# A decoder layer on 8 cores: the norm's scaling of tiles 8 to 15 on GpSimd, a new hand-written order, more zero products

## The chip, the cores and the metric

One Trainium2 chip, 8 cores, each with the same program on its own share of the data; the cores exchange nothing. The metric is the device time in microseconds of the slowest core. TensorE's clock has two levels in the records of this kernel, 1.2 and 2.4 GHz; the granted clock is given as a share of 2.4.

## The reference

One layer of a hybrid decoder on a prompt batch (8 sequences of 2048 tokens, one per core) and on a sample batch (128 sequences of 4 tokens, 16 per core), D = 1024:

```
h   = rmsnorm(x) * (1 + scale1) + shift1          # scale, shift, gate = silu(c) @ w_ada + b_ada
[v_pool | x_conv | B | C] = h @ w_in              # 4 x 512 columns
y_A = groupwise(mean_window(v_pool) - v_pool)     # windows 2, 4, 8, 16
y_B = B * dwconv3(C * x_conv)
x   = x + gate1 * rmsnorm([y_A | y_B] @ w_out)
h2  = rmsnorm(x) * (1 + scale2) + shift2
[a | b] = dwconv3(h2 @ w_up)                      # 2 x 2816 columns
x   = x + gate2 * rmsnorm((silu(a) * b) @ w_down)
```

The outputs are x and the last rows of the pooling, convolution and feed-forward inputs. All is float32 at the interface.

## The kernel before

A core holds its 2112 tokens as 17 tiles: 16 of 128 tokens and tile 16 with 64 sample tokens. Products are bfloat16 with float32 sums in PSUM, which has 8 banks of 512 columns.

**The first norm (T:t).** `tile_in(t)` calls `x_front(t)`, which loads x in pairs of tiles (1 MB, `load_pair`, on SP's queue; three pair buffers taken in turn, and a fourth place for the pair of tile 6), and `norm_tile` (L708). `stats` (L687) squares the tile on ScalarE with a sum, takes the root on ScalarE and the reciprocal on VectorE. Then the tile is scaled by it into a bfloat16 buffer: tiles 0 to 7 on VectorE (L730), tiles 8 to 16 on ScalarE (L728). `turn_tile` (L744) transposes the eight 128 x 128 blocks on TensorE into one PSUM bank, and VectorE or ScalarE copies them to AH, the transposed input of all projections. Buffers of the scaled tile: seven for tiles 0 to 7 (`xn` by t % 7), three for the others (t % 3).

**The start.** The scale vector's weights and the pooling columns of w_in come in 8 pieces (`scp`, 0.79 MB each at the source, cast by GpSimd's DMA queue). `a:kc` (`scale_in`) multiplies piece kc's part with silu(c) on TensorE, and VectorE makes the scale G1T of it. `s:kc,c` (`start_step`) applies it on VectorE to one block of 512 tokens (tiles 4c to 4c+3) and issues 4 (c = 0) or 3 (c = 1) start products of 512 columns (L856) that sum over kc in seven PSUM banks. These seven banks are held until s:7,c; tiles 0 to 2 and 4 to 6 are turned in the banks that c = 1 uses later, all others and every `a` take the one bank that is left, in the order of the list.

**The rest up to the output projection.** `O:g,c` copies a start bank out; `P:g,c` is a pooling projection of 8 products for a block of 512 tokens, `W:g,c` its window sums on VectorE; `m:j,c` issues the 24 products of a convolution unit (weights `ring<-w_inc`, 1.57 MB at the source), `v:j,c` its elementwise part, `U` both. `S` makes shift1 from four loads of 1 MB (`wsh`), `M:c` applies G1T to blocks 2 and 3, `A`, `g`, `G`, `Y`, `w` belong to the second modulation, the gates and the load of w_out, `F` folds the pooling map into w_out. Then `o_step` runs the output projection, and after it the feed-forward part.

**What sets the order.** The list PROJ (L48) says in which order these steps are recorded. That fixes the banks and buffers, and with them who waits for whom. `Sched.order` (L149) then plays the program through with written costs (DMA at 315e3 bytes per us, L144) and fixes each engine's queue: among what is ready, the lowest place in the list as TensorE uses it goes first. Loads are issued by the same rank, limited by the bytes in flight (L147); up to 70 us of the plan a load also waits for the load that had landed last when the plan issued it. All queues are in order on the chip: SP holds x loads, GpSimd the cast weight loads and its own arithmetic.

**Zero products.** `keep_warm` (L275) puts products with a tile of zeros ahead of a TensorE step that waits 0.5 us or more in the plan, up to 110 us: 0.85 of the gap, at 0.2139 us each (`PAD`, `FILL`, L273). They go to the bank that the step is about to write, as far as it has been freed, and wait for nothing that comes late. The start has 24 of them. The start product's padding (L861) exists as for other steps.

Each engine's queue is written out by `emit` (L307).

Of the kernel before, what the change touches and what calls it, by code (L numbers as in the profile page):

```python
# [12 lines left out]
ALU = mybir.AluOpType  # L13
# [3 lines left out]
KC = 8  # L17
T = 2048
# [74 lines left out]
class Sched:  # L93
# [176 lines left out]
                done(o)  # L270
        self.makespan = t

    PAD, FILL, PADDED = 0.2139, 0.85, 110.0  # L273

    def keep_warm(self, zeros):  # L275


        t = 0.0
        for o in self.ops["pe"]:
            gap, end = o.start - t, t  # L280
            t = o.start + o.cost
            if o.pad is None or gap < 0.5 or o.start > self.PADDED:
                continue
            late = {d for d in o.deps if d.end > end + 0.25 and d not in o.full}
            o.early = [d for d in o.deps - late if d.eng != "pe"] + [zeros]
            gap = o.start - max([end] + [d.end + self.HOP[d.eng] for d in o.full])
            o.pads = max(0, int(self.FILL * gap / self.PAD)) if end else self.FIRST
            zeros.need = True

    def finalize(self, esems, zeros):  # L290
        self.order()
        self.keep_warm(zeros)
        for o in self.all:
            if o.eng == "pe":
# [41 lines left out]
def build_program():  # L336
# [68 lines left out]
    STAT = alloc("stat", [128, 8, 18], F32)  # L405
# [50 lines left out]
    ZERO = alloc("zero", [128, 512], BF16)  # L456
# [36 lines left out]
    R = Region  # L493
# [369 lines left out]
    def tile_in(t):  # L863
        x_front(t)
# [790 lines left out]
```

How the kernel before makes its waits and increments, by code:

```python
    def emit(self, eng, e):  # L306
        waited = {}
        def wait(deps):
            need = {}
            for d in deps:
                s, v = d.sig
                if need.get(s, 0) < v:
                    need[s] = v
            for s, v in need.items():
                if waited.get(s, 0) < v:
                    e.wait_ge(s.h, v)
                    waited[s] = v
        for o in self.ops[eng]:
            if o.pads:
                wait(o.early)
                for _ in range(o.pads):
                    o.pad(e)
            wait(o.deps)
            if o.fn is None:
                continue
            r = o.fn(e)
            if o.dma:
                assert len(r) == o.n, (len(r), o.n)
                for i in r:
                    i.then_inc(o.sem.h, 16)
            elif o.need:
                r.then_inc(o.sig[0].h, 1)
```

## Time and profile before

| | |
|---|---|
| runs of the kernel before | 714.68, 716.30, 716.55 us, median 716.3 |
| the profiled execution | 716.71 us |
| its span, slowest core (core 1) | 715.2 us; the cores 710.0 to 715.2 |
| granted TensorE clock of the cores | 0.990 to 0.998 |
| busy: TensorE, VectorE, ScalarE, GpSimd | 691.9, 454.2, 318.9, 230.3 us |
| HBM read and written | 127.02 and 20.63 MB |

The profile is that of one execution on its slowest core; times in it are counted from the start of the span. The execution's own time is 1.5 us longer than the span. "PE" is TensorE's products, "PEld" its weight loads, "DVE" VectorE, "ACT" ScalarE, "POOL" GpSimd. Products are pipelined, so a group's time has the tail of its last product in it, and neighbouring groups overlap by some 0.17 us. The size in a line of the DMA view is that written to SBUF; a cast load reads twice as much.

### The profile page before, as it was taken

Reading aid. Unit: us, or ns where it says so; the run is one execution under the profiler, and the core shown is the slowest. Engines: PE = TensorE matmul, PEld = TensorE weight load, DVE = VectorE, ACT = ScalarE, POOL = GpSimd, SP = SyncE. Lnnn points to the kernel's source line nnn. Section 1 sums busy time; section 2 is a strip of 40 time slices with the busy share of each in tenths; the row PEclk is TensorE's granted clock in tenths of the full one; section 3 lists DMA queues with packets and bytes.
Section 4 is the critical chain, followed back from the end, with each engine's and each line's share of the span. In section 5 each row is a group of like instructions: output and inputs, shape, how many; then the busy total and the mean of one; then the engine's idle time right before and its main releaser. Section 6 shows DMA issues by size and latency. Waiting matters only on the chain.

```text
span 715.2 us, 11905 instructions; the slowest of 8 cores (710.0 to 715.2 us)
## 1 busy us (share of the span) xinstructions
PE 691.9 (97%) x4022; PEld 329.2 (46%) x4022; DVE 454.2 (64%) x612; ACT 318.9 (45%) x600; POOL 230.3 (32%) x231
## 2 busy tenths in 40 slices
PE   6889999999899999999999999999999999999996
PEld 2435544444444444444444444454444444444443
DVE  2729599664688787777777333157777777769303
ACT  4258654334576864444444211154444445423111
POOL 1100012000777743344444222214324242323320
PEclk8999999999999999999999999999999999999998
DMA  8998879999998579358999968103244333062322
GB/s 233 213 230 140 204 133 172 163 176 177 216 236 307 188 132 164 60 110 143 156 158 162 221 194 266 60 31 74 51 95 78 60 59 60 1 238 98 127 88 75
DMA packets 31980, 102.81 MB, mean 144 GB/s; under 512 B 11632, under 2 KB 12144, under 8 KB 27056
## 3 DMA queue, kind: packets, MB, share of 16 engines
q0 software_dynamic: 9072, 47.71, 39.8%
q1 hardware_dynamic: 22848, 54.33, 25.1%
q8 instruction: 33, 0.54, 0.3%
q14 instruction: 27, 0.22, 0.1%
HBM read 127.02 MB, written 20.63 MB: 206 GB/s over the span
## 4 chain that ended last, share of the span: by engine, by line
PE 90%; issue 3%; DVE 2%; ACT 2%; POOL 1%; DMA 1%; DVEq 0%; SPq 0%; ACTq 0%; POOLq 0%
PE ps L541 84%; PE ps L856 2%; PE ps L551 1%; PE ps L534 1%; PE ps L559 1%; DMA big<-x 1%; DVE big L576 1%; POOL big L580 1%; ACT xnp L572 1%; DVE ah L757 1%; POOL e L580 0%; ACT big L572 0%; DVE stat L691 0%; ACT stat L572 0%; ACT L572 0%
## 5 line engine op out<-in xcount | busy, mean ns | idle before, releaser
L541 PE MATMUL ps<-ah,ring 128*128 128x512 bf16 (+2 forms) x2240 | 405.3, 342 | 1.6 <-DVE big L576 0.8
L541 PEld LDWEIGHTS ps<-ah,ring 128*128 128x128 bf16 x2240 | 188.2, 98 | 212.5 <-issue 4.3
L576 DVE SCALAR_TENSOR_TENSOR big<-ps,misc,big 128x1023 f32<-128x1023 f32 (+1 forms) x176 | 224.9, 1282 | 73.2 <-ACT halo L572 30.7
L580 POOL TENSOR_TENSOR g<-big 128x1024 bf16<-128x1024 f32 x44 | 104.5, 2375 | 173.6 <-DVE big L580 96.3
L572 ACT ACTIVATE big<-ps,misc 128x1024 f32<-128x1024 f32 x88 | 97.9, 1114 | 139.8 <-PE ps L541 139.8
L541 PE MATMUL ps<-wdn,g 128*128 128x512 bf16 (+2 forms) x726 | 153.1, 373 | 0.0
L541 PEld LDWEIGHTS ps<-wdn,g 128*128 128x128 bf16 x726 | 69.9, 98 | 81.1 <-issue 0.4
L580 POOL TENSOR_TENSOR big<-big 128x256 f32<-128x256 f32 (+2 forms) x35 | 52.9, 1522 | 110.7 <-DVE big L576 97.1
L572 ACT ACTIVATE big<-ps 128x1024 bf16<-128x1024 f32 (+4 forms) x31 | 29.0, 937 | 122.8 <-PE ps L541 106.6
L691 DVE RECIPROCAL stat<-stat 128x1 f32<-128x1 f32 (+1 forms) x64 | 9.9, 159 | 96.3 <-ACT stat L572 96.0
L541 PE MATMUL ps<-wo,by 128*128 128x512 bf16 x256 | 57.0, 379 | 1.4 <-DVE stat L691 1.4
L572 ACT ACTIVATE big<-big 128x1024 f32<-128x1024 f32 x44 | 46.5, 1056 | 4.3 <-DVE big L580 3.3
L541 PEld LDWEIGHTS ps<-wo,by 128*128 128x128 bf16 x256 | 24.6, 98 | 30.2 <-issue 2.3
L591 POOL DMA_DIRECT2D ring<-w_up x22 | 12.8, 581 | 75.8 <-PE ps L541 75.8
L576 DVE SCALAR_TENSOR_TENSOR big<-ps,stat,gtp 128x1024 f32<-128x1024 f32 x26 | 33.3, 1281 | 5.4 <-PE ps L541 3.3
L576 DVE SCALAR_TENSOR_TENSOR ta<-q,misc,ta 128x512 f32<-128x512 f32 x32 | 23.7, 748 | 7.8 <-ACT q L572 2.6
L572 ACT ACTIVATE junk<-big 128x1024 bf16<-128x1024 f32 (+1 forms) x15 | 15.7, 1049 | 20.0 <-DMA big<-x 20.0
L534 PE MATMUL ps<-zero 128*128 128x512 bf16 x74 | 21.0, 428 | 3.7 <-DVE zero L602 1.9
L572 ACT ACTIVATE stat<-stat,eps 128x1 f32<-128x1 f32 (+1 forms) x64 | 17.4, 291 | 2.5 <-ACT big L572 0.4
L541 PE MATMUL ps<-ah,scp 128*128 128x512 bf16 (+1 forms) x104 | 18.0, 322 | 0.0
L587 DVE TENSOR_SCALAR ah<-ah,g2t,s2t 128x512 bf16<-128x512 bf16 x32 | 15.4, 541 | 2.9 <-DMA ah<-xnp 2.9
L580 DVE TENSOR_TENSOR tsa<-usb,misc 128x1408 f32<-128x1408 f32 x6 | 13.6, 2273 | 5.6 <-ACT usb L572 5.4
(150 smaller groups left out, 461.1 us busy)
## 6 DMA issues: line engine op xcount, KB each, us to landing
ring<-w_up POOLq DMA_DIRECT2D x22, 1024.0 KB, 10.0
y<-big SPq DMA_DIRECT2D x23, 512.0 KB, 2.8
big<-y SPq DMA_DIRECT2D x16, 512.0 KB, 4.7
big<-x SPq DMA_DIRECT2D x7, 1024.0 KB, 8.0
wdn<-w_down POOLq DMA_DIRECT2D x11, 512.0 KB, 12.2
wg<-w_gate POOLq DMA_DIRECT2D x4, 1024.0 KB, 15.7
big<-x SPq DMA_DIRECT2D x8, 512.0 KB, 11.1
scp<-w_scp POOLq DMA_DIRECT2D x8, 384.0 KB, 7.1
```

Source lines behind the costliest of these rows:

```text
L534: o.pad = lambda e: e.matmul(ap, ZERO[:, 0:ap.shape[0]], ZERO[:, 0:n], start=first, stop=first)
L541: inst = e.matmul(bank_ap, l, r, start=(first and i == 0), stop=(last and i == len(pairs) - 1))
L551: inst = e.matmul(o, ls[i], r, start=(i == 0), stop=(i == len(ls) - 1))
L559: inst = e.transpose(o, i, ident)
L572: return K.op("act", lambda e: e.activation(out=out, in_=in_, func=func, **kw), reads=reads, writes=writes, cost=c_act(n, ptr))
L576: return K.op("dve", lambda e: e.scalar_tensor_tensor(out, in0, s, in1, op0, op1), reads=reads, writes=writes, cost=c_dve(n), port=not any ...
L580: return K.op(eng, lambda e: e.tensor_tensor(out, in0, in1, op), reads=reads, writes=writes, cost=c_dve(n) if eng == "dve" else c_pool(n), ...
L587: return K.op("dve", lambda e: e.tensor_scalar(out, in0, s1, s2, op0, op1), reads=reads, writes=writes, cost=c_dve(n, mode), port=mode > 1.0)
L591: return K.dma(eng, lambda e: [e.dma_start(out=dst, in_=src)], sem or next_misc(), 1, reads=reads, writes=regs, deps=deps, nbytes=nbytes)
L691: K.op("dve", lambda e: e.reciprocal(STAT[0:rows, k + 1, t:t + 1], STAT[0:rows, k + 1, t:t + 1]), reads=[r_stat[k + 1][t]], writes=[r_stat ...
L757: K.op("dve", lambda e: e.tensor_copy(AH[:, :, r0:r0 + rows], psb[:, :, 0:rows]), reads=[r_bank[b]], writes=regs, cost=c_dve(KC * rows, 2.0))
L856: inst = e.matmul(PSF[:, start_b[g, c], :], WINP[kc][:, g * 128:(g + 1) * 128], AH[:, kc, c * 512:(c + 1) * 512], start=(kc == 0), stop=(k ...
```

## The change

It does four things. The scaling of tiles 8 to 15 goes from ScalarE to GpSimd (tile 16 stays on ScalarE). The list PROJ is another one. A second play-through, `retime`, keeps the order of the queues and sets the planned times anew with slower DMA (295e3 bytes per us) and 0.05 us more for each hand-over between engines; the number of zero products follows from these times. `keep_warm` fills 0.9 of a gap in place of 0.85, and between s:0,0 and s:7,0 it fills every planned gap of 0.35 us or more, ahead of any TensorE step, with zero products that are added to the first start bank and wait for nothing but the zeros.

```diff
 PROJ = """
-T:0 T:1 T:2 a:0 T:6 T:3 T:7 T:4 a:1 T:5 a:2 s:0,0 s:1,0 a:3 a:4 s:0,1 s:2,0 a:5 T:8 s:1,1 s:3,0 s:2,1 s:4,0
-s:3,1 T:9 a:6 a:7 s:5,0 s:6,0 s:7,0 s:4,1 O:1,0 s:5,1 O:0,0 s:6,1 s:7,1 T:10 m:0,1 T:11 O:2,0 O:2,1 T:16 M:2 K
-m:0,0 W:0,0 T:12 W:2,0 S O:3,0 W:1,0 m:0,4 O:1,1 P:3,1 O:0,1 W:3,0 v:0,0 P:2,2 P:0,2 W:2,1 m:1,0 I T:13 T:14
-m:1,4 v:1,0 m:0,2 W:3,1 P:1,2 T:15 W:1,1 v:0,1 M:3 P:3,2 v:0,2 m:1,1 W:0,1 Z W:2,2 W:1,2 v:1,1 m:0,3 P:1,3 N
...
+T:0 T:1 T:2 T:10 T:11 T:3 a:0 T:6 T:14 s:0,0 T:12 a:1 a:2 T:7 T:4 a:3 a:4 s:1,0 T:5 T:13 s:0,1 s:2,0 a:5 a:6
+s:3,0 s:1,1 s:2,1 a:7 s:4,0 s:5,0 s:6,0 s:3,1 s:7,0 K O:2,0 W:2,0 O:0,0 s:4,1 T:15 m:0,0 s:5,1 O:1,0 s:6,1 T:16
+s:7,1 T:8 T:9 O:2,1 O:1,1 W:1,0 O:3,0 S m:0,4 P:3,1 W:2,1 M:2 W:3,0 O:0,1 m:1,4 v:0,0 m:0,1 P:1,2 P:2,2 W:0,0
+M:3 m:0,3 P:0,2 C m:1,0 v:1,0 Y:1 W:0,1 v:0,1 m:0,2 I v:0,2 Y:0 W:1,1 P:0,3 m:1,1 v:1,1 W:2,2 N W:3,1 v:0,4
...
 """
+XPOOL = tuple(range(8, 16))
...
+    SLOW, LATE = 295e3, 0.05
+
+    def retime(self):
...
-    PAD, FILL, PADDED = 0.2139, 0.85, 110.0
+    PAD, FILL, PADDED = 0.2139, 0.9, 110.0
 
     def keep_warm(self, zeros):
...
         t = 0.0
+        hot = None
         for o in self.ops["pe"]:
             gap, end = o.start - t, t
             t = o.start + o.cost
+            if o is self.hot[1]:
+                hot = None
+            if o is self.hot[0]:
+                hot = self.hot[2]
+            elif hot is not None and gap >= 0.35:
+                o.pad, o.early, o.pads = hot, [zeros], int(self.FILL * gap / self.PAD)
+                zeros.need = True
+                continue
...
         self.order()
+        self.retime()
         self.keep_warm(zeros)
...
-        if k == ST1 and t > 7:
+        if k == ST1 and t in XPOOL:
+            K.op("pool", lambda e: e.tensor_scalar(N[0:rows, :], X[0:rows, :], STAT[0:rows, k + 1, t:t + 1], None, ALU.mult),
+                 reads=[r_x, r_stat[k + 1][t]], writes=[r_n], cost=1.3)
+        elif k == ST1 and t > 7:
             act(N[0:rows, :], X[0:rows, :], AF.Copy, [r_x, r_stat[k + 1][t]], [r_n], D, scale=STAT[0:rows, k + 1, t:t + 1])
...
-        return padded(o, PSF[:, start_b[gs[0], c], :], 512, kc == 0)
+        padded(o, PSF[:, start_b[gs[0], c], :], 512, kc == 0)
+        if c == 0 and kc in (0, KC - 1):
+            hot.append(o)
...
+    K.hot = hot + [lambda e: e.matmul(PSF[:, start_b[0, 0], :], ZERO[:, 0:128], ZERO, start=False, stop=False)]
     K.finalize(esems, zeros)
```

The later lines of the list differ too; the weights of the second modulation, of w_out and the last convolution units keep their place behind the first 100 us.

## Rows read from the trace of the kernel before

**Rows 1.** The page: its span and TensorE's busy time.

```profile
span 715.2 us, 11905 instructions; the slowest of 8 cores (710.0 to 715.2 us)
...
PE 691.9 (97%) x4022; PEld 329.2 (46%) x4022; DVE 454.2 (64%) x612; ACT 318.9 (45%) x600; POOL 230.3 (32%) x231
```

**Rows 2.** Stretches: window, length, busy PE, PEld, DVE, ACT, POOL, granted clock, DMA share, GB/s.

```profile
40.50:54.57 14.07, 11.19 (x68) 5.39 (x67) 3.42 (x10) 7.30 (x13) 1.05 (x2) 0.88 1.01 246
54.57:95.60 41.03, 40.31 (x354) 21.80 (x353) 31.31 (x67) 30.26 (x67) 3.26 (x7) 1.00 0.80 152
95.60:169.80 74.20, 74.13 (x505) 35.76 (x506) 56.70 (x100) 31.45 (x85) 6.01 (x13) 1.00 0.99 175
```

**Rows 3.** The same view for the zero products alone (PE, PEld).

```profile
9.00:54.57 45.57, 14.13 (x50) 4.96 (x50) 0.89 1.02 226
```

**Rows 4.** TensorE's timeline, core 1: start, duration, operation, [idle before <- releaser].

```profile
40.55 3.40 PE L534 MATMUL ps<-zero 128*128 128x512 bf16 x15
43.78 0.61 PE L559 MATMUL ps<-idb,xn 128*128 128x128 bf16 x8
...
45.55 0.61 PE L559 MATMUL ps<-idb,xn 128*128 128x128 bf16 x8
47.43 0.34 PE L541 MATMUL ps<-sc,scp 128*128 128x18 bf16 x8 [1.27 <-ACT ah L572]
...
48.79 4.87 PE L856 MATMUL ps<-ah,scp 128*128 128x512 bf16 x14
...
54.57 0.61 PE L559 MATMUL ps<-idb,xn 128*128 128x128 bf16 x8
55.02 5.34 PE L541 MATMUL ps<-ah,ring 128*128 128x512 bf16 x24
...
85.35 1.89 PE L541 MATMUL ps<-ah,ring 128*128 128x512 bf16 x8 [0.70 <-DVE bias L1023]
```

**Rows 5.** Loads: when issued (timelines of GpSimd and SP), then us to landing (DMA view).

```profile
33.83 0.53 POOL L591 DMA_DIRECT2D scp<-w_scp  x1 [1.69 <-DMA scp<-w_scp]
39.33 0.53 POOL L591 DMA_DIRECT2D ring<-w_inc  x1 [4.98 <-DMA scp<-w_scp]
...
36.66 0.33 SPq L591 DMA_DIRECT2D big<-x  x1
...
scp<-w_scp POOLq DMA_DIRECT2D x1, 384.0 KB, 7.4
...
big<-x SPq DMA_DIRECT2D x1, 1024.0 KB, 7.5
ring<-w_inc POOLq DMA_DIRECT2D x1, 768.0 KB, 9.8
```

**Rows 6.** ScalarE's timeline: the square and the scaling of tile 8.

```profile
36.68 1.06 ACT L572 ACTIVATE junk<-big 128x1024 bf16<-128x1024 f32 x1 [12.83 <-DMA big<-x]
...
39.32 1.15 ACT L572 ACTIVATE xn<-big,stat 128x1024 bf16<-128x1024 f32 x1
```

**Rows 7.** TensorE's timeline of core 2: the last start products, first products of m:0,0.

```profile
47.01 3.18 PE L856 MATMUL ps<-ah,scp 128*128 128x512 bf16 x14
...
51.56 4.70 PE L541 MATMUL ps<-ah,ring 128*128 128x512 bf16 x21
```

**Rows 8.** TensorE's waits on other engines, 55 to 170 us: total, times, longest.

```profile
PE ps L541 <- DVE bias L1023: 0.7, 1, 0.7
```

**Rows 9.** Groups of instructions by shape: busy us, mean ns, idle before.

```profile
L572 ACT ACTIVATE xn<-big,stat 128x1024 bf16<-128x1024 f32 x8 | 9.2, 1146 | 1.2 <-DVE stat L691 1.1
...
L585 DVE TENSOR_SCALAR xn<-big,stat 128x1024 bf16<-128x1024 f32 x6 | 4.2, 747 | 0.0
...
L580 POOL TENSOR_TENSOR g<-big 128x1024 bf16<-128x1024 f32 x44 | 104.5, 2375 | 173.6 <-DVE big L580 96.3 <-DVE big L576 69.8 <-DVE hc L580 4.1
L580 POOL TENSOR_TENSOR big<-big 128x1024 f32<-128x1024 f32 x14 | 36.5, 2604 | 94.7 <-DVE big L576 84.6 <-DMA big<-y 10.1
```

**Rows 10.** The tile view of g2t: ns min/median/max of the modulations beside GpSimd's additions.

```profile
L587 DVE TENSOR_SCALAR ah<-ah,g2t,s2t x32: 388/402/1391, 204.1 to 435.6; 128x512 bf16<-128x512 bf16 x32
```

More of the change, by code:

```diff
@@ L48 @@
 PROJ = """
-T:0 T:1 T:2 a:0 T:6 T:3 T:7 T:4 a:1 T:5 a:2 s:0,0 s:1,0 a:3 a:4 s:0,1 s:2,0 a:5 T:8 s:1,1 s:3,0 s:2,1 s:4,0
-s:3,1 T:9 a:6 a:7 s:5,0 s:6,0 s:7,0 s:4,1 O:1,0 s:5,1 O:0,0 s:6,1 s:7,1 T:10 m:0,1 T:11 O:2,0 O:2,1 T:16 M:2 K
-m:0,0 W:0,0 T:12 W:2,0 S O:3,0 W:1,0 m:0,4 O:1,1 P:3,1 O:0,1 W:3,0 v:0,0 P:2,2 P:0,2 W:2,1 m:1,0 I T:13 T:14
-m:1,4 v:1,0 m:0,2 W:3,1 P:1,2 T:15 W:1,1 v:0,1 M:3 P:3,2 v:0,2 m:1,1 W:0,1 Z W:2,2 W:1,2 v:1,1 m:0,3 P:1,3 N
-W:3,2 P:2,3 m:1,2 W:2,3 W:1,3 v:0,3 W:0,2 C Y:1 Y:0 P:0,3 v:1,2 W:0,3 P:3,3 R v:0,4 L W:3,3 W:1,4 m:1,3 v:1,3 B
-W:3,4 A:6 U:2,4 A:7 w U:2,0 U:3,4 U:2,1 U:3,0 U:3,1 A:1 A:0 A:2 U:3,2 U:2,2 g v:1,4 W:2,4 U:3,3 A:4 A:5 A:3 G
-W:0,4 F U:2,3
+T:0 T:1 T:2 T:10 T:11 T:3 a:0 T:6 T:14 s:0,0 T:12 a:1 a:2 T:7 T:4 a:3 a:4 s:1,0 T:5 T:13 s:0,1 s:2,0 a:5 a:6
+s:3,0 s:1,1 s:2,1 a:7 s:4,0 s:5,0 s:6,0 s:3,1 s:7,0 K O:2,0 W:2,0 O:0,0 s:4,1 T:15 m:0,0 s:5,1 O:1,0 s:6,1 T:16
+s:7,1 T:8 T:9 O:2,1 O:1,1 W:1,0 O:3,0 S m:0,4 P:3,1 W:2,1 M:2 W:3,0 O:0,1 m:1,4 v:0,0 m:0,1 P:1,2 P:2,2 W:0,0
+M:3 m:0,3 P:0,2 C m:1,0 v:1,0 Y:1 W:0,1 v:0,1 m:0,2 I v:0,2 Y:0 W:1,1 P:0,3 m:1,1 v:1,1 W:2,2 N W:3,1 v:0,4
+P:2,3 W:1,2 P:3,2 g W:3,2 v:1,4 R P:1,3 P:3,3 W:0,2 Z L A:6 v:0,3 W:1,3 m:1,2 v:1,2 W:3,3 U:2,4 U:2,0 A:3 m:1,3
+A:7 W:3,4 U:2,1 v:1,3 W:0,3 U:2,2 U:3,4 U:2,3 A:2 W:2,3 U:3,0 A:0 U:3,1 B W:1,4 A:1 A:5 W:0,4 U:3,2 w F A:4
+W:2,4 G U:3,3
 """
@@ L271, in order, with push, done @@
         self.makespan = t
-    PAD, FILL, PADDED = 0.2139, 0.85, 110.0
+    SLOW, LATE = 295e3, 0.05
+    def retime(self):
+        users = {o: [] for o in self.all}
+        wait = {o: len(o.deps) for o in self.all}
+        for o in self.all:
+            for d in o.deps:
+                users[d].append(o)
+        turn = {e: 0 for e in self.ENGS}
+        busy = {e: False for e in self.ENGS}
+        queue = {"sp": [], "pool": []}
+        events = []
+        seq = [0]
+        port = [0.0, 0.0]
+        t = 0.0
+        ready = {o for o in self.all if not wait[o]}
+        left = len(self.all)
+        def push(at, kind, o):
+            seq[0] += 1
+            heapq.heappush(events, (at, seq[0], kind, o))
+        def done(o):
+            o.end = t
+            for u in users[o]:
+                wait[u] -= 1
+                if not wait[u]:
+                    push(t + (0.0 if o.eng == u.eng == "pe" else self.HOP[o.eng] + self.LATE), "ready", u)
+        while left:
+            for e in self.ENGS:
+                if busy[e] or turn[e] >= len(self.ops[e]) or self.ops[e][turn[e]] not in ready:
+                    continue
+                o = self.ops[e][turn[e]]
+                turn[e] += 1
+                busy[e] = True
+                o.start = t
+                c = o.cost
+                if o.dma:
+                    push(t + c, "free", o)
+                    continue
+                if o.port:
+                    c += max(0.0, port[e != "pool"] - t)
+                    port[e == "pool"] = t + c
+                push(t + c - self.OVER[e], "free", o)
+                push(t + c, "done", o)
+            live = [q for q in queue.values() if q]
+            nxt = events[0][0] if events else 1e9
+            head = None
+            rows = sum(q[0][0].row for q in live)
+            for q in live:
+                f = t + q[0][1] * rows / (self.SLOW * q[0][0].row)
+                if f <= nxt:
+                    nxt, head = f, q
+            for q in live:
+                q[0][1] -= (nxt - t) * self.SLOW * q[0][0].row / rows
+            t = nxt
+            if head is not None:
+                push(t + self.DMA_OUT, "landed", head.pop(0)[0])
+                continue
+            _, _, kind, o = heapq.heappop(events)
+            if kind == "ready":
+                ready.add(o)
+            elif kind == "free":
+                busy[o.eng] = False
+                left -= 1
+                if o.dma:
+                    push(t + self.DMA_IN, "moving", o)
+            elif kind == "moving":
+                queue[o.eng].append([o, float(o.nbytes)])
+            else:
+                done(o)
@@ L281, in keep_warm @@
             t = o.start + o.cost
+            if o is self.hot[1]:
[5 more added lines that the diff above has]
+                zeros.need = True
+                continue
             if o.pad is None or gap < 0.5 or o.start > self.PADDED:
@@ L848, in start_weights @@
         load(SCP[kc], wsp_d[kc], [r_scp[kc]], 3 << 18, eng="pool")
+    hot = []
     def start_mm(kc, c):
```

## The prediction

> **What bounds the kernel now.** I first read the page: TensorE is busy for 691.9 of 715.2 us [rows 1]. The time is TensorE's instruction stream plus what is lost in it, so a change in the order pays only where TensorE runs zero products, waits, or runs at the lower clock. The stretches say where that is [rows 2]: from 95.6 to 169.8 us TensorE is busy for 74.13 of 74.20 us, from 54.57 to 95.6 us 0.7 us are missing, while the last 14 us before 54.57 hold 2.9 us of idle time at a granted clock of 0.88. The zero products lie in the same place: 50 of them with 14.13 us between 9 and 54.57 us [rows 3]. What the change can win lies before 55 us, some 0.7 us of it behind.
>
> TensorE's timeline shows how the stretch ends [rows 4]. 15 zero products run from 40.55 us, the transposes of T:8 start at 43.78, those of T:9 at 45.55, and only then a:6 at 47.43. a:6 itself was long ready: scp 7, the last of its kind, was issued at 33.83 and took 7.4 us, so it was there at 41.2 [rows 5]. It waited because T and a share the one PSUM bank that the start products leave free, in the order of the list, and T:8, T:9 stand ahead of it. T:8 is late because its x pair landed at 36.7 us (ScalarE had waited 12.83 us for it) and its tile was scaled at 40.47 [rows 6]; the 15 zero products then held it for 3.3 us more. The 14 start products after that took 4.87 us, in core 2 3.18 us: they ran at the 1.2 GHz level for a part of it, after the gaps of 44 to 48.8 us. Core 2 started its first product of m:0,0 at 51.56 us and core 1, the slowest, at 55.02 [rows 4, 7]; their spans are the 710.0 and 715.2 us of the page.
>
> **The new order.** T:10 to T:14 come ahead of a:7, and T:8, T:9 behind s:7,1. The bank chain of a:6 and a:7 then hangs on x pairs loaded early, so the stop of 40.5 to 48.8 us cannot recur in this form. But seven pairs of x (0, 2, 10, 6, 14, 12, 4) now land before scp 7, where it was five and part of a sixth.
>
> What the transfers allow: by 41.2 us had landed misc 0.24 MB, five x pairs of 1.05 MB, eight scp of 0.79 MB (f32 at the source) and some 0.63 MB of the pair issued at 36.66 (7.5 us) [rows 5]: 12.4 MB in 40.1 us, 0.309 MB/us. The same sum to the landing of w_inc (39.33 + 9.8 us = 49.1) gives 15.1 MB in 48.0 us, 0.314. I take 0.312. In the new order scp 7 makes 13.87 MB, so 46 us; a:7, its VectorE steps and the last seven start products take about 3 us, which is 49. m:0,0 needs w_inc 0 too: 15.44 MB, with the samples' tile and half of the pair of T:8 moving beside it (0.8 MB, as its neighbours did before) 16.24 MB: 52.1 + 1.1 = 53.1 us. T:15 and T:16 fill 0.8 us of the time between.
>
> The terms, for core 1:
> - m:0,0 starts at 53.1 in place of 55.0 us: -1.9. The cold start products are in this, for TensorE has slack before w_inc lands.
> - By then 14 tiles and the samples are turned, before only T:0 to T:10. Three tiles at 0.45 us (54.57 to 55.02 us [rows 4]) and, my estimate from that, 0.35 for the samples: -1.7.
> - The 0.70 us wait at 85.35 [rows 4] was for a bank that VectorE freed late, beside T:14. T:14 is gone from there: -0.7.
> - More zero products. They run for 0.9 of each planned gap, with a plan that moves 0.295 MB/us, 5.5% under my measured 0.312. Where the data comes earlier than planned they hold real work, as the 15 did. At 16.24 MB the plan is 3.0 us behind, of which 0.9 are filled: the bound is 2.7 us, the other end 0 (TensorE waits anyway and stays warm). I take +0.5, nearer to 0 since w_inc's landing and not TensorE ends this stretch.
> - ScalarE loses eight scalings of 1.146 us, 9.2 in all [rows 9]. Between 55 and 170 us TensorE's one wait is the 0.7 us on VectorE, none is on ScalarE [rows 8], so this is worth nothing; what hides it is TensorE's full stream.
> - GpSimd gains eight scalings, which no row shows. VectorE does one in 0.747 us, GpSimd's own products of 1024 columns take 2.375 and 2.604 us [rows 9]; I take 2.4, the same engine and output type. Six of them (tiles 10 to 15) fall before 49 us, between the scp loads of the same queue. A load in flight covers 7.4 us, so I put the delay at nothing; without that cover it is the second rival.
>
> The pair of T:4 now waits for the buffer of 10 and 11, which GpSimd frees: landing at 18 to 19 us plus two scalings is 25 us, and the transfers reach that pair (9.94 MB) only at 33 us. T:4 can start about 37 us. From there to 47 us TensorE has some 9.6 us of real work for 10 us: tight, and the first place where the forecast can slip. VectorE, SP's queue and the output projection see the same work earlier, at no cost that I can name; behind 170 us nothing changes but the start.
>
> GpSimd's price by the Trainium skill, GPSIMD Engine Reference, section 3.1, would be smaller: its two-input products stand at a port floor that one-input work escapes, down to 1.8 cycles per element, an estimate of 1.5 us for 1024. The trace agrees with the two-input figure only (2.375 us); no row has the other. By it six scalings are 9 us, and the second rival loses most of its price.
>
> Sum: -1.9 - 1.7 - 0.7 + 0.5 = -3.8 us. The profiled execution took 716.7 us (span 715.2 and 1.5 around it), so 712.9; it lies 0.4 above the median of 716.3, so **712.5 us**. About 0.3%, 2.1 us, is what a measurement of this kernel can tell from no change.
>
> **Rivals.**
> 1. Zero products eat it. The plan's slower transfers are obeyed by real instructions: +2.7 in place of +0.5 gives a gain of 1.6, 714.7 us. For it: both groups of zero products that I looked at ran on after their tile was ready. Against it: the last wait is a load. Chance 0.18.
> 2. The GpSimd queue. Loads stand behind scalings that wait for x and for VectorE's reciprocal. Six scalings of 2.4 us, 14.4, less the cover of 7.4 us, put scp 7 and w_inc 0 7.0 us later: m:0,0 at 60.1 us, 5.1 later than now, less 2.4 for the tiles and the bubble: 2.7 us slower, 719.0 us. It decides from 4 us of idle transfers before 50 us. Chance 0.15.
> 3. The shared port. One VectorE scaling of 512 columns took 1391 ns where the shortest took 388, beside GpSimd's adds [rows 10]: 1.0 us of blocking. Eight new GpSimd instructions could each cost a VectorE step on the chain that; if half of them hit, 4.0 us: 716.5 us. Chance 0.06. The Trainium skill, SBUF — State Buffer, section Who interferes with whom, states this as a rule (the port pair is locked for a whole instruction, the second one blocks fully), and the trace agrees [rows 10]; before the output projection the old kernel had no GpSimd arithmetic to collide with.
> 4. The loads arrive better than that: w_inc 0 not slowed by its neighbours (15.44 MB, 50.6 us) and no pad held: 3.0 us more gain, 709.5 us. Chance 0.07.
> 5. The planner reorders, and the list comes out much as before: 716.3 us, 0.02. The bank chain follows the list itself, which speaks against it.
>
> **How the numbers follow.** The forecast has 0.52, with its own range of 710.5 to 714.1. Faster by over 0.3% is 0.52 + 0.07, within 0.3% 0.18 + 0.06 + 0.02, slower 0.15. The range reaches from below the fourth rival to just inside the second: 708.5 to 718.
>
> **What would show it.** Right: a:6 and a:7 within 2 us of scp 7's landing at 46 us; no half-clock stretch between 20 and 55 us; m:0,0 at 53 us with 14 tiles turned; more than 60 zero products before 55 us; no TensorE wait at 85 us; GpSimd scalings of 1.5 to 2.5 us. Wrong: TensorE standing before T:4 beyond 38 us, idle transfers before 50 us, VectorE steps of over 1 us, or new gaps between 55 and 170 us, which would give the gain back where it is full now.

## The result and the profile after

The changed kernel took 729.7 us (median of 4 runs, 728.7 to 731.2) against 716.3 us for the kernel before: a ratio of 1.018 (95% interval 1.016 to 1.020), 13 us slower. The forecast was 712.5 us, 3.8 us faster. In some executions, whatever the kernel, the cores of one die show a lower granted clock and the time is some per cent longer; the ratios leave these out. The page and the groups by shape of the changed kernel, slowest core (core 2):

```profile
span 727.7 us, 11911 instructions; the slowest of 8 cores (717.0 to 727.7 us)
PE 696.1 (96%) x3974; PEld 332.6 (46%) x4049; DVE 458.7 (63%) x612; ACT 312.2 (43%) x592; POOL 254.6 (35%) x239
L815 POOL TENSOR_SCALAR xn<-big,stat 128x1024 bf16<-128x1024 f32 x8 | 23.6, 2956 | 17.6 <-DVE stat L778 15.0
```

Against [rows 1] TensorE is busy 4 us longer and idle 8 us longer. GpSimd's scaling takes 2.96 us in the mean. That is more than the 2.4 us that I took, and more than the 2.604 us of its slowest product [rows 9]. The stretches say where TensorE loses time; the columns are those of [rows 2]:

```profile
24.00:40.50 16.50, 11.72 (x79) 6.39 (x82) 5.50 (x13) 4.17 (x9) 9.88 (x7) 0.79 0.81 169
40.50:54.57 14.07, 12.25 (x112) 6.51 (x113) 10.80 (x26) 6.16 (x13) 8.53 (x8) 1.00 0.70 113
54.57:70.00 15.43, 14.19 (x85) 6.74 (x85) 10.89 (x29) 8.99 (x19) 2.08 (x4) 1.00 0.79 174
169.80:215.00 45.20, 40.27 (x203) 18.41 (x206) 23.43 (x36) 22.15 (x49) 19.25 (x26) 0.92 0.75 142
```

Two places stand out. From 40.5 to 54.57 us the DMA share is 0.70 where it was 1.01 [rows 2], and from 169.8 to 215 us TensorE is idle for 4.9 us and has a clock of 0.92. From 24 us on the DMA share is lower as well. The kernel before had these two lines (core 1), and was idle for 2.9 us in the second:

```profile
24.00:40.50 16.50, 13.66 (x120) 7.25 (x119) 8.88 (x26) 3.66 (x7) 2.77 (x7) 1.00 1.05 202
169.80:215.00 45.20, 42.26 (x230) 20.06 (x229) 28.22 (x48) 26.31 (x58) 28.21 (x38) 1.00 1.01 214
```

**The first place, before m:0,0.** The chain of waits of the changed kernel from 24 us on (start, duration, what), cut to its long pieces:

```profile
26.95 13.83 DMA big<-x
...
40.86 1.20 ACT junk L659 x3
...
44.66 1.05 ACT junk L659 x2
...
46.36 1.04 PE ps L948 x4
...
47.45 1.76 POOL xn L815
...
50.78 2.90 POOL xn L815
53.68 9.40 DMA ring<-w_inc
63.08 0.14 issue
63.22 0.81 PE ps L628 x3
```

It reads backwards: m:0,0 starts at 63.22 us, when w_inc 0 has landed; that load was issued at 53.68, when the last two scalings were done. GpSimd's timeline of the same core shows who stands ahead of whom:

```profile
20.34 5.67 POOL L815 TENSOR_SCALAR xn<-big,stat 128x1024 bf16<-128x1024 f32 x2 [10.17 <-DVE stat L778]
25.97 1.12 POOL L678 DMA_DIRECT2D scp<-w_scp  x2
...
44.31 0.53 POOL L678 DMA_DIRECT2D scp<-w_scp  x1 [1.25 <-DMA scp<-w_scp]
47.45 6.28 POOL L815 TENSOR_SCALAR xn<-big,stat 128x1024 bf16<-128x1024 f32 x2 [2.61 <-PE ps L948]
53.68 0.58 POOL L678 DMA_DIRECT2D ring<-w_inc  x1
```

GpSimd delays the loads at two points. The scalings of tiles 10 and 11 hold its queue until 26.0 us, and the next two scp loads stand behind them: they go out at 24.3 to 26.0 us in the eight cores, where the first of them goes out at 21.1 to 22.4 when GpSimd scales nothing (13). Later the last pair of scalings starts at 47.45 us and takes 6.28, and w_inc 0, issued at 39.33 before [rows 5], goes out 14.4 us later, at 53.68. In all cores it goes out at 51.4 to 53.7.

What the last pair waited for differs. In core 2, the slowest, the x pair of T:4 landed late, at 40.8 us, the statistics of the last tiles stood behind those of T:4 in ScalarE's queue, and the chain above goes through them. In the seven other cores the pair starts at 45.2 to 46.3 us. In cores 0, 3, 5 and 6 ScalarE had the last statistics done by 40.9 to 42.3, and the scalings waited for VectorE's reciprocals. In core 0 these stood in VectorE's queue behind a step that waited 1.44 us for TensorE's `a`:

```profile
43.21 0.29 DVE L674 TENSOR_SCALAR g1t<-ps,vd,misc 128x17 f32<-128x17 f32 x1 [1.44 <-PE ps L628]
...
44.81 0.22 DVE L778 RECIPROCAL stat<-stat 128x1 f32<-128x1 f32 x2
```

The x load of T:4 was not held up by the buffer that GpSimd frees: it goes out at 26.7 to 27.6 us in all cores, and at 28.2 to 29.3 when GpSimd scales nothing (13).

The DMA view of 10 to 64 us in 40 slices of 1.35 us (busy tenths, then GB/s) has both holes:

```profile
DMA  7999999999940699999998793699998000899998
GB/s 261 358 292 165 273 290 316 370 340 340 340 158 0 73 164 132 163 199 229 266 244 171 70 203 59 91 125 155 148 203 160 5 0 5 118 197 255 256 352 364
```

Nothing moves from 26.2 to 27.5 us, and almost nothing from 51.9 to 55.9 us, around the issue of w_inc 0.

**GpSimd once more, at T:9.** The scalings of tiles 8 and 9 come behind s:7,1, and TensorE waits for the second of them:

```profile
71.46 5.97 POOL L815 TENSOR_SCALAR xn<-big,stat 128x1024 bf16<-128x1024 f32 x2
77.58 0.61 PE L646 MATMUL ps<-idb,xn 128*128 128x128 bf16 x8 [2.40 <-POOL xn L815]
```

Every core has this wait of 2.3 to 2.6 us. Where GpSimd scales nothing, or only half the columns, it is not there.

**The second place, the output projection.** TensorE's timeline in core 2, then SP's:

```profile
178.32 10.52 PE L628 MATMUL ps<-wo,by 128*128 128x512 bf16 x47
193.57 9.99 PE L628 MATMUL ps<-wo,by 128*128 128x512 bf16 x32 [4.72 <-DVE stat L778]
```

```profile
176.71 0.33 SPq L678 DMA_DIRECT2D e<-x  x1
177.68 0.81 SPq L1277 DMA_DIRECT2D gtp<-gate_scratch  x2
178.53 3.21 SPq L1279 DMA_DIRECT2D gts<-gate_scratch  x2
```

The gate is loaded at 177.68 us, 0.64 us ahead of the first output product (before: issued at 167.09 in core 1, 2.7 us ahead). VectorE needs it for the first residual, so it waits 8.2 us, the PSUM banks stay taken, and TensorE stands 4.72 us. Behind the stall 32 products take 9.99 us, 0.31 each, where 47 took 10.52 before it: the granted clock from 193.57 to 203.5 us is 0.70, so it was at the 1.2 GHz level for a part of them. Two things hold the load back. The new list puts A:4 behind F, and the gate lies over the buffer of A:4's weights; and in SP's queue it stands behind the load `e<-x`. They were lifted together (6), so how much each costs is not shown. The first output product itself comes at 175.5 to 180.4 us, before at 167.3 to 169.8.

The cores split by this stall without any experiment: 0, 5 and 6 have none there and spans of 717.0 to 718.7 us; 1, 2, 3, 4 and 7 stand 1.7 to 4.7 us and have 724.3 to 727.7.

### The profile page after: what moved, and what is told of

Its sections match the earlier page's. It is cut to its first block, busy times and chain, and to the rows that moved or that the text cites. A ratio compares the mean times of both kernels' runs of the same rounds, so it can differ in the third digit from the quotient of the medians.

```text
span 727.7 us, 11911 instructions; the slowest of 8 cores (717.0 to 727.7 us)
## 1 busy us (share of the span) xinstructions
PE 696.1 (96%) x3974; PEld 332.6 (46%) x4049; DVE 458.7 (63%) x612; ACT 312.2 (43%) x592; POOL 254.6 (35%) x239
## 4 chain that ended last, share of the span: by engine, by line
PE 79%; DMA 8%; issue 4%; DVE 3%; ACT 3%; POOL 2%; SPq 0%; DVEq 0%; ACTq 0%; POOLq 0%
PE ps L628 77%; DMA big<-x 4%; DMA gts<-gate_scratch 2%; DVE big L663 1%; DMA ring<-w_inc 1%; DMA scp<-w_scp 1%; PE ps L638 1%; POOL xn L815 1%; DVE ah L674 1%; ACT big L659 1%; ACT junk L659 0%; POOL big L667 0%; ACT xnp L659 0%; PE ps L646 0%; ACT stat L659 0%
## 5 line engine op out<-in xcount | busy, mean ns | idle before, releaser
L667 POOL TENSOR_TENSOR big<-big 128x256 f32<-128x256 f32 (+2 forms) x35 | 52.9, 1519 | 110.2 <-DVE big L663 96.4
L628 PE MATMUL ps<-wo,by 128*128 128x512 bf16 x250 | 59.2, 393 | 5.0 <-DVE stat L778 4.7
L678 POOL DMA_DIRECT2D ring<-w_up x22 | 12.8, 582 | 70.5 <-DMA gts<-gate_scratch 53.1
L815 POOL TENSOR_SCALAR xn<-big,stat 128x1024 bf16<-128x1024 f32 x8 | 23.6, 2956 | 17.6 <-DVE stat L778 15.0
L646 PE MATMUL ps<-idb,xn 128*128 128x128 bf16 (+1 forms) x140 | 12.0, 238 | 11.6 <-POOL xn L815 6.1
L847 DVE COPY ah<-ps 128x1024 bf16<-128x1024 bf16 (+1 forms) x17 | 11.4, 670 | 16.8 <-PE ps L646 16.7
L621 PE MATMUL ps<-zero 128*128 128x512 bf16 (+1 forms) x61 | 18.0, 454 | 2.9 <-DVE zero L689 1.9
```

The lines of the kernel that those rows point to most:

```text
L621: o.pad = lambda e: e.matmul(ap, ZERO[:, 0:ap.shape[0]], ZERO[:, 0:n], start=first, stop=first)
L628: inst = e.matmul(bank_ap, l, r, start=(first and i == 0), stop=(last and i == len(pairs) - 1))
L646: inst = e.transpose(o, i, ident)
L667: return K.op(eng, lambda e: e.tensor_tensor(out, in0, in1, op), reads=reads, writes=writes, cost=c_dve(n) if eng == "dve" else c_pool(n), ...
L678: return K.dma(eng, lambda e: [e.dma_start(out=dst, in_=src)], sem or next_misc(), 1, reads=reads, writes=regs, deps=deps, nbytes=nbytes)
L815: K.op("pool", lambda e: e.tensor_scalar(N[0:rows, :], X[0:rows, :], STAT[0:rows, k + 1, t:t + 1], None, ALU.mult), reads=[r_x, r_stat[k + ...
```

## The experiments

Theory A: GpSimd's scaling delays m:0,0. Theory B: the late gate load costs the rest. Rivals: the zero products; the loss of ScalarE's part; the new list itself. "The order as it stands" below means that the planner's result for the changed kernel is written into the kernel, so that every queue keeps its order. "o" is the first output product, "up" the first up-projection product; the time between is 60.8 us when TensorE stands nowhere in it.

**1. The new list without GpSimd.**

```diff
-XPOOL = tuple(range(8, 16))
+XPOOL = ()
```

> The changed kernel with tiles 8 to 15 scaled by ScalarE again; GpSimd's queue is then the same list of loads with the eight scalings taken out. Theory A (loads wait behind scalings in GpSimd's queue): m:0,0 starts at 53 to 55 us instead of 60.6 to 63.3, DMA share back to 0.95 or more between 24 and 54 us, total 718 to 721 us, since the late gate load at the output projection stays. Rival B (the new order of the x pairs is itself to blame): m:0,0 still at 59 us or later and the total above 725 us. Rival C (zero products): the same as B, for they stay.

Ratio 1.013 (1.011 to 1.015). m:0,0 comes at 55.7 to 57.8 us, some 5 us earlier than with GpSimd. But TensorE stood 0.4 to 4.0 us on the weights `w_ss` at 131 to 137 us in every core, and 0.8 to 4.1 us at the output projection in five cores; the three that did not stand there (1, 2 and 5) have spans of 713.1 to 713.8 us. GpSimd is a part, not all.

**2. GpSimd's scaling in the old list.**

```diff
+        if k == ST1 and t > 7 and t < 16:
+            K.op("pool", lambda e: e.tensor_scalar(...), ..., cost=1.3)
```

> The kernel before with tiles 8 to 15 scaled by GpSimd, old list, old zero products. Theory A: slower than before by some 3 to 8 us, with the loads behind the scalings late (fewer scalings stand ahead of the scp loads in the old list, only those of tiles 8 and 9, so less than in the changed kernel). Rival B and rival C: within 1 us of before. In no theory a wait of over 2 us at the output projection beyond what before had.

Ratio 1.009 (1.006 to 1.012): the scaling on GpSimd alone costs 6.4 us in the old list, with four scalings of 2.84 us before 60 us in core 4. The cause is another one here than in the changed kernel. w_inc 0 stands ahead of the scalings in this queue and goes out at 39.2 to 41.6 us, as before. TensorE waits 4.0 to 5.6 us for the scaled tiles themselves (cores 0, 4, 6), and m:0,0 is 2.5 us later in the mean; the rest is lost behind it, under a plan that was made anew. So this run prices the scaling in front of TensorE, and says nothing of loads behind it.

**3. An earlier gate by the list.**

```diff
-... B W:1,4 A:1 A:5 W:0,4 U:3,2 w F A:4
+... B W:1,4 A:1 A:4 A:5 W:0,4 U:3,2 w F
```

> The changed kernel with one step of the list moved: A:4 stands behind A:1 in place of behind F, so the gate vector's buffer is free earlier and its load (G) can be issued some 8 us before the output projection. Theory A with the second part D (the first tail of the output projection waits for the gate load): 3 to 5 us less than the changed kernel, 725 to 727 us, the VectorE wait on the gate load gone, the start of the output projection where it was. Rival E (the stall there is ScalarE's and VectorE's backlog): no change, 729 to 730.

Ratio 1.027 (1.025 to 1.029), slower than the changed kernel. The stall at the output projection was gone (61.9 us from o to up), but the planner made a new plan of everything behind it, and 490 us passed from "up" to the end where the changed kernel has 481. An edit of the list is not a clean experiment in this kernel; from here on the order is kept.

**4. The old number of zero products.**

```diff
-        self.retime()
+        pass
-    PAD, FILL, PADDED = 0.2139, 0.9, 110.0
+    PAD, FILL, PADDED = 0.2139, 0.85, 110.0
```

(The filling of every planned gap between s:0,0 and s:7,0 is out too.)

> The changed kernel with the zero products of before (0.85 of a gap from the first play-through, no filling between s:0,0 and s:7,0), every queue else in the same order. Theory A: within 2 us of the changed kernel, since loads end that stretch; the half-clock level may last longer. Rival C (zero products hold real work): at least 4 us faster than the changed kernel.

Ratio 1.017 (1.014 to 1.020), the changed kernel 1.018: no price to be seen.

**5. Scalings of half the length.** The order as it stands.

```diff
-e.tensor_scalar(N[0:rows, :], X[0:rows, :], STAT...
+e.tensor_scalar(N[0:rows, 0:512], X[0:rows, 0:512], STAT...
```

> The changed kernel with every queue, bank, wait and zero product as it is, but GpSimd scales 512 of the 1024 columns of tiles 8 to 15 (the other half of the products' input is left out), so that one scaling takes about 1.4 us, what the plan had assumed, in place of 2.83. Theory A (scalings that are longer than planned hold back the loads behind them): m:0,0 at 57 to 59 us in place of 60.6 to 63.3, DMA share between 24 and 54 us above 0.9, total 724 to 726 us. Rival B (the order is to blame, whatever GpSimd takes): m:0,0 after 60.5 us, total 728 or more.

GpSimd scales only the first 512 columns of tiles 8 to 15 here. A scaling takes 1.55 us, m:0,0 is at 55.4 to 58.3 us, the ratio 1.004 (1.002 to 1.006): 10 of the 13 us hang on the scaling's length, be it in the queue or in front of TensorE. Stalls of 1.1 to 4.8 us at the output projection remain.

**6. The gate load alone.** The order as it stands but for one entry of SP's queue: the gate load stands right behind the store of `ncs`. Its buffer lies over weights that are used earlier:

```diff
+    W2[1], W2[4] = W2[4], W2[1]
-        if kc < 4:
+        if kc in (0, 2, 3, 4):
             for r in r_xnp:
```

> The changed kernel with its order of all queues frozen, except: the gate load G stands three loads earlier in SP's queue, and the weights of A:1 and A:4 have exchanged places in memory, so that G no longer waits for the last A. Theory D (the first tail waits for the gate load): the load issued at 166 to 170 us, no VectorE wait over 1 us at the output projection in any core, from the first output product to the first product of the up projection 61 us in all cores in place of 61 to 68.6, total 725 to 727 us, and, other than in the run where the plan was made anew, no new wait after 240 us. Rival E (VectorE's backlog): the wait stays.

Ratio 1.009 (1.006 to 1.012). The load went out 12.2 us ahead of the first output product, and every core took 60.8 us from o to up. TensorE's timeline of the slowest core (core 5):

```profile
181.89 17.43 PE L637 MATMUL ps<-wo,by 128*128 128x512 bf16 x80
```

80 products without a stop at 0.218 us each. Theory B holds, with 6.7 us. m:0,0 stayed at 60.2 to 63.3 us.

**7. The old list with the new zero products.** The kernel before with `retime`, 0.9 and the filling between s:0,0 and s:7,0.

```diff
+T:0 T:1 T:2 a:0 T:6 T:3 T:7 T:4 a:1 T:5 ...   (the list of before)
+XPOOL = ()
```

> The kernel before (its list, ScalarE's scaling) with the new zero products alone: second play-through, 0.9 of a gap, filling from s:0,0 to s:7,0 (17, 5 and 6 of them around T:8 and T:9 in place of 15 and 1, 7 ahead of T:10 in place of 5). Rival C (zero products are a real cost): 1 to 3 us slower than before. Theory A: within 1.5 us of before; the half-clock stretch of 48 to 53 us gone, which gives back about what the added ones take.

Ratio 1.000 (0.998 to 1.001).

**8. Fewer zero products in the kernel before**, one in place of the 15 ahead of T:8 and of the 5 ahead of T:10.

```diff
+            if o.pads in (15, 5) and o.start > 35.0:
+                o.pads = 1
```

> The kernel before with 1 zero product ahead of T:8 in place of 15 and 1 ahead of T:10 in place of 5. If they held ready work, as the rows of before read, T:8 runs 3 us earlier and m:0,0 starts at 51 to 52 us: 2 to 3.5 us faster than before, unless the half-clock stretch grows by the same. The latter is the rival: no change.

Ratio 0.999 (0.997 to 1.002). m:0,0 came at 51.2 to 54.6 us, 1.6 us earlier in the mean. The 14 start products behind took 4.5 to 5.9 us, partly at the lower clock (granted 0.64 to 0.88 from 40.5 to 54.57 us in the cores, 0.76 to 1.00 before); in the kernel before they took 3.2 to 6.1. The mean span of the cores is 1.3 us shorter in the profiled execution, but the slowest cores (0, 3 and 4) stood 0.3 to 2.0 us for the gate at the output projection, and the time did not change measurably. With 4 and 7 this settles the zero products: neither more nor fewer of them changed the kernel's time.

**9. Both causes out.** Experiments 5 and 6 together; as in 5, columns 512 to 1023 of tiles 8 to 15 are not written.

> Both earlier cuts at once: the changed kernel's order, GpSimd scaling half the columns of tiles 8 to 15 (1.4 us each; the other half of the products' input is left out), and the gate load early. If the length of the scalings and the late gate load are the two causes and add up, the total is that of f2_half_scaling less the 3 to 5 us of its stall: 714 to 718 us, no more than 0.3% from before. If something else in the new order costs time too, it stays above 719.

Ratio 0.997 (0.996 to 0.999): the two account for all that the change lost, and 2 us more: 15 us are regained with both out, where one alone regains 10 and 6.7, so they overlap a little. The half scaling takes out the wait at T:9 too.

**10. GpSimd's queue in another order.** Experiment 6, and in GpSimd's queue scp 1 ahead of the scaling of tile 11, scp 4 ahead of that of tile 12, w_inc 0 between the last two.

```diff
-q[i:i+17]=[12,51,57,13,14,79,15,88,16,257,297,17,18,19,123,170,20]
+q[i:i+17]=[12,51,13,57,14,79,15,16,88,17,18,19,257,297,123,20,170]
```

(51, 57, 79, 88, 123 and 170 are scalings, 257 and 297 memsets, the others loads. The three last scp loads also go ahead of the two memsets, and the scaling 88 behind scp 3.)

> The changed kernel with full scalings on GpSimd and the gate load early; in GpSimd's queue alone, five places are changed so that loads go ahead of scalings that they do not need: scp 1 ahead of the scaling of tile 11, scp 4 ahead of that of tile 12, scp 5 to 7 ahead of two memsets that wait for VectorE, w_inc 0 ahead of the last scaling of its pair. Theory A: the scp loads are issued 2 to 3 us earlier, m:0,0 starts 2 to 3 us earlier than in f1_gate (60 to 63 us), total 720 to 723 us in place of 724. If GpSimd's price is the port or the time of T:13 and not the queue: no change against f1_gate.

Ratio 1.013 (1.010 to 1.015), against 1.009 in 6. w_inc 0 went out at 49.4 to 52.2 us in place of 51.4 to 52.8, and m:0,0 still came at 60.9 to 64.0. A load moved ahead of one scaling gains only that scaling, and the scaling then stands behind the load: the last one ended at 52.9 to 55.7 us, in 6 at 51.4 to 52.9. The expected 2 to 3 us did not come; whether the order is worse than that of 6 is at the edge of what the intervals tell.

**11. Experiment 6 with ScalarE's scaling**, on experiment 1's plan.

> e1_scalar (the new list, ScalarE's scaling) with its queues frozen and the gate load early. The stall of 3.6 us on it at the output projection goes: 721 to 723 us in place of 726. What is left above before is the new list's own price: m:0,0 2 us later and the wait of up to 4 us near 136 us for the second modulation's weights.

Ratio 1.006 (1.004 to 1.008), experiment 1 had 1.013. "o" was at 171.1 to 177.6 us. TensorE stood again for `w_ss`, 0.6 to 3.2 us in every core; this wait is the likely rest, and it was not taken out by itself.

**12. The kernel before with an earlier gate load.** Experiment 8, and the store of the gate rows three x loads earlier.

```diff
+    q=ops['sp']; q.remove(550); q.insert(q.index(617)+1,550)
```

> The kernel before with 1 zero product ahead of T:8 and T:10 each (as b1_fewer_zeros) and, in SP's queue, the store of the gate row ahead of three x loads that it had waited behind (one of them for another store to land). The gate load then goes 3 to 4 us earlier, the stall at the output projection is gone in all cores, and the slow cores of b1_fewer_zeros (714) come near its fast ones (708.5): 710 to 712 us, 5 us faster than before. If the gate load is not what its slow cores wait for: 716, as b1_fewer_zeros.

Ratio 1.000 (0.999 to 1.002). The gate load went out 7.1 us ahead of the first output product in every core, some 3 us earlier than in 8. But its first part now took 11.3 to 14.2 us to land in cores 0, 2 and 5 (the last part up to 16.3; before 9.0 to 11.6), and four cores (0, 2, 5 and 7) still stood 0.6 to 2.1 us.

**13 and 14. VectorE does the scaling, and a spare GpSimd instruction keeps the queue.** Both on experiment 6. 13 moves the eight scalings to VectorE, right behind the reciprocals; 14 adds a GpSimd scaling of the same size in each old place, from a constant tile into a spare buffer.

```diff
-            K.op("pool", lambda e: e.tensor_scalar(N[0:rows, :], X[0:rows, :], ...
+            ts(N[0:rows, :], X[0:rows, :], STAT[0:rows, k + 1, t:t + 1], None, ALU.mult, ...   # 13 and 14
+            K.op("pool", lambda e: e.tensor_scalar(SPARE, MISC[:, 0:256]..., STAT[...], ...),  # 14
+                 reads=[r_x, r_stat[k + 1][t], r_cts], writes=[r_spare], cost=1.3)
```

> The changed kernel's queues as they stand, with the gate load freed as in f1_gate, and the eight scalings of tiles 8 to 15 done by VectorE (0.75 us each) instead of GpSimd; nothing is left out. Theory (GpSimd's 2.8 us scaling and the late gate load are all that the change lost): as in g1_half_gate, m:0,0 at 55 to 58 us, 714 to 717 us, a ratio of 0.995 to 1.000. Rival (the new order asks VectorE for more than it has before 55 us): VectorE becomes the wait before 50 us, m:0,0 at 60 us, a ratio of 1.005 or more, so that the scaling has no good place in this order.

> g4_vector_gate, with a GpSimd scaling of 1024 columns into a spare buffer in each of the eight places of its queue where the scaling stood, waiting for the same load and the same reciprocal and holding the same x buffer; TensorE does not wait for it. If the loads behind the scalings in GpSimd's queue, or the shared port, cost the time, m:0,0 is at 60.2 to 63.3 us as in f1_gate and the ratio near 1.009. If it is the length of the scaling in the chain of the tiles (g2_loads_first_gate points there), m:0,0 stays within 1.5 us of g4_vector_gate and the ratio within 0.002 of its. Between the two, the difference to each is its share.

Of the first runs of these two, cores 0 to 3 are compared. The slowest of the four took 715.6 us in 13 and 717.1 in 14 (medians over the executions), against 714.0 in the kernel before. Both kernels were run once more:

> The kernel of g4_vector_gate once more, since four of the eight cores ran at a mean clock of 0.94 in all executions of that call and of the kernel before beside it. From the four other cores there (slowest of them 715.6 us against 714.0) a ratio of 1.000 to 1.004 if GpSimd and the gate load are all that the change lost apart from VectorE's own load; below 0.998 if the disturbed die hid a gain like that of g1_half_gate; above 1.006 if VectorE is the new wait.

> The kernel of g5_vector_spare once more, for the same reason. There m:0,0 was at 57 to 59 us in four cores and at 63 to 63.6 in the other four, a mean of 60.5 us against 57.4 with the GpSimd queue free. If the queue and the port carry the greater part, the same split shows again and the ratio lies 0.003 to 0.006 above g6_vector_again; if the split came from the disturbed die, all cores are within 1.5 us of g6_vector_again.

13 gives 0.998 (0.996 to 1.000), 14 gives 1.006 (1.004 to 1.008). In 13 the transfers never stop in the stretch of 10 to 64 us. Its DMA view (core 5), with the same slices as above:

```profile
DMA  9999999999999998899998898889999899989999
```

w_inc 0 goes out at 43.1 to 45.8 us and m:0,0 starts at 56.6 to 58.4. In 14 the cores fall apart; core, span and clock:

```profile
core 0: 712.8 us, clock 0.992
core 1: 719.3 us, clock 0.991
core 2: 712.0 us, clock 0.996
core 3: 722.1 us, clock 0.990
core 4: 717.1 us, clock 0.992
core 5: 712.7 us, clock 0.994
core 6: 718.7 us, clock 0.992
core 7: 712.0 us, clock 0.997
```

and GpSimd's timeline, core 2 and then core 3, tells them apart:

```profile
42.02 3.33 POOL L830 TENSOR_SCALAR tb<-misc,stat 128x1024 bf16<-128x1024 f32 x1
45.52 3.18 POOL L830 TENSOR_SCALAR tb<-misc,stat 128x1024 bf16<-128x1024 f32 x1 [0.17 <-POOL tb L830]
48.65 0.58 POOL L688 DMA_DIRECT2D ring<-w_inc  x1
```

```profile
49.20 0.53 POOL L688 DMA_DIRECT2D scp<-w_scp  x1 [4.15 <-DVE xn L682]
49.76 2.85 POOL L830 TENSOR_SCALAR tb<-misc,stat 128x1024 bf16<-128x1024 f32 x1
52.78 3.05 POOL L830 TENSOR_SCALAR tb<-misc,stat 128x1024 bf16<-128x1024 f32 x1 [0.17 <-POOL tb L830]
55.78 0.58 POOL L688 DMA_DIRECT2D ring<-w_inc  x1
```

Where w_inc 0 went out by 50.2 us (cores 0, 2, 5, 7), m:0,0 came at 57.5 to 58.7 and the span is 712.0 to 712.8 us, as in 13. Where it went out at 51.8 to 55.8 us, m:0,0 came at 62.2 to 66.4 and the span is 717.1 to 722.1. So w_inc 0 can go out some 5 us later than in 13 (43.1 to 45.8 us) at no cost, and from there on each microsecond of the queue counts. In ratios: 1.009 with the scaling in the chain (6), 1.006 with a scaling beside it (14), 0.998 without (13). 0.008 of the 0.011, about three quarters, need no tile to wait for GpSimd; they come from its queue and from the port. The other quarter is the scaling in front of TensorE. The intervals of 6 and 14 overlap, but the wait itself is seen: every core of 6 stands 2.4 to 2.6 us for the scaling of T:9, and no core of 14 does. How the three quarters divide between queue and port was not tried, nor a plan made anew with the scaling's true cost.

## Why the prediction was wrong

**The step that failed first: "I put the delay at nothing; without that cover it is the second rival."** The second rival's mechanism came true. Its number, m:0,0 at 60.1 us where 60.6 to 63.3 were measured, is partly luck: it was added up from a start at 53.1 us and a delay of 7.0, and measured were 57.6 us without GpSimd and a delay of 4.2 (means of the cores). Its total of 719.0 us was too low, for it had no gate load and no wait at T:9 in it. Two things were wrong with the cover. The scaling takes 2.83 us alone and 3.14 beside VectorE's work, not 2.4. And a load in flight covers a scaling only if the scaling is ready when the load goes out. The last two were not: they waited for their reciprocals until 45.2 to 47.5 us, with scp 7 already out, and the whole pair of 6.28 us stood ahead of w_inc 0. The rival's "4 us of idle transfers before 50 us" came as 1.3 us at 26 and 4.0 us at 52.

**"Six of them".** The sum counts the scalings of tiles 10 to 15 and leaves those of tiles 8 and 9 at nothing, without a reason. They cost TensorE 2.3 to 2.6 us at T:9 in every core.

**T:4.** "Landing at 18 to 19 us plus two scalings is 25 us, and the transfers reach that pair only at 33 us": the scalings did end at 26.0, and the pair's load went out at 26.7 to 27.6 us. It landed at 35.7 to 37.1 us in four cores, near enough to my 37 for the start of T:4, and at 38.9 to 40.9 in the four others (35.4 to 37.3 in all cores without GpSimd's scaling, 1 and 13). I had named this as the first place to slip, and looked for the loss on TensorE. In core 2 it went through ScalarE's queue to the last scalings instead, 1 to 2 us of their start against the other cores; in cores 0, 3, 5 and 6 it had no part in it.

**m:0,0 at 53.1 us.** It would have been wrong without GpSimd too, where it is 56.6 to 58.4 (13). I let three microseconds of TensorE's work follow scp 7. TensorE's timeline of 13 (core 5) shows what follows it:

```profile
45.49 1.06 PE L655 MATMUL ps<-idb,xn 128*128 128x128 bf16 x16
46.38 1.67 PE L1640 MATMUL ps<-zero 128*128 128x512 bf16 x7
48.13 0.81 PE L957 MATMUL ps<-ah,scp 128*128 128x512 bf16 x3
...
53.05 2.53 PE L957 MATMUL ps<-ah,scp 128*128 128x512 bf16 x11
55.42 0.61 PE L655 MATMUL ps<-idb,xn 128*128 128x128 bf16 x8
55.87 2.11 PE L957 MATMUL ps<-ah,scp 128*128 128x512 bf16 x9
57.81 7.07 PE L637 MATMUL ps<-ah,ring 128*128 128x512 bf16 x32
```

40 start products (3 + 7 + 10 + 11 + 9) and three `a` stand behind two tiles that are turned at 45.5: 9.7 us from 48.1 to 57.8. I had counted bytes to the end and TensorE's work only up to 47 us.

**The tiles turned ahead and the 0.7 us wait (-2.4).** The work ahead is real: from m:0,0 to the first output product the kernel before takes 114.9 us in the mean of its cores (53.8 to 168.7), 13 takes 113.3 (57.6 to 170.9). That is 1.6 us of the 2.4. But the output projection still starts 2.2 us later than before.

**"Behind 170 us nothing changes but the start."** The second failed step. I had read TensorE's waits only up to 170 us [rows 8] and followed no load of SP's queue behind that. Moving A:4 and the x loads moved the gate load too, and the stall that follows it is worth 6.7 us (6). The kernel before already stands there (1.45 us in core 1): its cores take 62.8 us from o to up in the mean, with the gate early it is 60.8. These 2.0 us bring 9 and 13 back to the level of before; they pay for the 2.2 us just named. Without the gate's edit the new list was slower with the scaling on ScalarE (1.013) and on GpSimd (1.018); on VectorE it was run only with that edit.

**Zero products (+0.5, bound 2.7).** Nothing was measured (4, 7), so the first rival falls. That 15 of them held T:8 back by 3.3 us is worth no measurable time either (8): m:0,0 came 1.6 us earlier in the mean, and the kernel took as long.

**ScalarE's eight scalings.** I put their loss at nothing, and ahead of m:0,0 nothing is seen of it: with them on ScalarE (1) it is at 55.7 to 57.8 us, with them on VectorE (13) at 56.6 to 58.4. Behind it no run separates them.

**The port.** The third rival's blocking is real. Six of VectorE's modulations beside the GpSimd pair took 4.02 us (from 49.85 us), the same six in 13 took 1.67: 2.35 us in one place. How much of it lies on the chain no run separates. The tile view of g1t, ns min/median/max:

```profile
L672 DVE TENSOR_SCALAR ah<-ah,g1t x16: 343/352/1196, 31.8 to 58.1; 128x512 bf16<-128x512 bf16 x16
```

A few are blocked for up to 0.85 us, the others not at all; in 13 the same view reads 346/348/354. The Trainium skill, SBUF — State Buffer, section Who interferes with whom, says that the second one blocks fully; the trace agrees in kind, but a blocked step here waited for less than a third of a 3.1 us GpSimd instruction.

**GpSimd's price by the page.** The Trainium skill, GPSIMD Engine Reference, section 3.1, gives 1.8 cycles per element as the best case of one-input work, an estimate of 1.5 us. Here 1024 columns took 2.83 us and 512 took 1.55, nearly twice that; I was right not to use it, but my own 2.4 us, from the two-input products, was too low as well.

Of the signs that I listed as wrong, "VectorE steps of over 1 us" and a new gap between 55 and 170 us (T:9) came in full, "idle transfers before 50" in part, and "T:4 beyond 38 us" in some cores. Of the signs of being right, the scalings of 1.5 to 2.5 us and the full clock between 20 and 55 us failed (2.83 us; granted 0.79 from 24 to 40.5 us in core 2).

## What to carry to other kernels

- When an engine whose queue also issues loads is given arithmetic, list its queue in order and ask for each instruction when its inputs are there. An instruction that waits holds every load behind it for its wait and its length. Here a later w_inc 0 was free for some 5 us (14), and all beyond that was paid; what such slack is worth has to be worked out, and not taken as the whole.
- A moved step moves the loads that need its buffer or stand behind it in a queue. Follow it to all buffers that lie over one another, up to the next stage, count every instruction that moved (here eight scalings, not six), and look at the first wait after the stretch that is changed.
- In a kernel whose plan is computed, hold the order fixed when one thing is to be tested.

## What the runs showed of the hardware

- GpSimd's multiplication by a per-partition scalar, float32 to bfloat16, 128 x 1024: 2.83 us alone and up to 3.3 us beside VectorE's work, 128 x 512: 1.55 us. It was slower than its product of two inputs of the same shape (2.37 us), which I had taken for the dearer one.
- A small load through a scratch in HBM (the gate, to all partitions) landed after 3.1 us (3) to 14.2 us (12), its last part after up to 16.3. Issuing it some 3 us earlier (12) bought nothing; that the traffic beside it makes the difference was not tested by itself.
- TensorE's clock fell to the 1.2 GHz level behind a stall of 4.7 us in the midst of a full stream (47 products in 10.52 us ahead of it, 32 in 9.99 behind it at a granted clock of 0.70); a part of a stall's price is paid in the products that follow it.
